# Mixture-of-experts stage: routing joined to the expert steps, first transfers reordered, output gain applied to expert rows

## What is computed

```python
x = x + g1 * mix
h = rms_norm_2(x, ffn_norm_g[layer]) * (1 + sc2) + sh2
ffn = moe(h, router_w, router_b, ex_w1[layer], ex_w3[layer], ex_w2[layer])
x = x + g2 * ffn

# in moe: 16 experts in 4 groups of 4; best group, then its best 2 experts
scores = jax.nn.sigmoid(h2 @ router_w)
...
y = (jax.nn.silu(xb @ w1[e]) * (xb @ w3[e])) @ w2[e]     # per row, 1024 -> 512 -> 1024
return y * g[:, None]                                     # gate of the row, then summed per token
```

## Time and profile before

| | us |
|---|---|
| median of three runs | 4971.45 |
| the profiled execution | 4973.66 |
| its span, first to last instruction | 4972.0 |
| routing and start of steps, layer 0 | 3304 to 3395 |
| expert steps, layer 0 | 3395 to 3887 |
| combine, layer 0 | 3887 to 3946 |
| routing and start of steps, layer 1 | 4346 to 4437 |
| expert steps, layer 1 | 4437 to 4930 |
| combine, layer 1 | 4930 to 4972 |

### The profile page before, as it was taken

How to read it: one execution, slowest core, us unless ns; L and a number is a source line. 1 busy time by engine, 2 the same in 40 slices (tenths; PEclk the granted TensorE clock), 3 DMA queues, 4 the chain that set the end, 5 groups by cost and what they waited for, 6 DMA issues and landing times. The chain is left out here.

```text
span 4972.0 us, 59425 instructions
## 1 busy us (share of the span) xinstructions
PE 4175.6 (84%) x20947; PEld 2139.8 (43%) x20947; DVE 1899.6 (38%) x2939; ACT 1138.8 (23%) x1872; POOL 261.4 (5%) x366
## 2 busy tenths in 40 slices
PE   3699699998999998999588978856999599939995
PEld 0355355555444445777444435432333244413331
DVE  1233344443312205998535837431111423321113
ACT  0122355443111112222020236210111235101111
POOL 0000000000000000111000000000000200000001
PEclk7799899999999998999799989978999799969997
DMA  6322311113355511111240130334864511266656
GB/s 254 115 67 62 69 38 38 36 36 123 120 197 207 207 57 47 53 53 52 95 155 9 55 115 26 100 141 185 327 253 167 186 29 54 98 254 241 241 228 258
DMA packets 261229, 627.23 MB, mean 126 GB/s; under 512 B 73837, under 2 KB 153789, under 8 KB 241257
## 3 DMA queue, kind: packets, MB, share of 16 engines
q1 hardware_dynamic: 222194, 508.17, 28.9%
q0 software_dynamic: 19424, 94.01, 5.1%
q10 hardware_dynamic: 19480, 23.31, 1.4%
HBM read 1298.33 MB, written 113.53 MB: 284 GB/s over the span
## 5 line engine op out<-in xcount | busy, mean ns | idle before, releaser
L3425 PE MATMUL blocks_h<-od_hT,blocks_xT 128*32 128x512 f32 x1280 | 288.3, 604 | 74.6 <-ACT blocks_xT L3368 67.5
L1645 PE MATMUL hyp_acc<-hy_hT,hyp_early_weights 128*128 128x512 f32 x768 | 335.0, 594 | 0.0
L3425 PE MATMUL blocks_h<-moe_w,blocks_xT 128*32 128x512 f32 x2560 | 295.5, 615 | 27.1 <-issue 27.1
L3446 PE MATMUL blocks_acc<-moe_w,blocks_hidT 128*32 128x512 f32 x2560 | 285.8, 598 | 10.0 <-DMA moe_w<-in_ex_w 10.0
L3425 PE MATMUL blocks_h<-moe_w1b,blocks_xT 128*32 128x512 f32 x1280 | 288.3, 604 | 0.0
L970 PE MATMUL att_scores<-att_kT,att_qT 64*128 64x512 f32 (+3 forms) x768 | 251.6, 547 | 22.2 <-DMA att_v<-scratch_V 22.2
L700 PE MATMUL lat_acc<-lat_w_in,lat_hT 128*128 128x512 f32 (+1 forms) x640 | 244.6, 538 | 2.5 <-DMA lat_w_in<-in_attn_w_in 2.5
L2209 PE MATMUL evp_acc<-ev_hT,evp_early_weights 128*128 128x512 f32 x512 | 224.6, 599 | 7.6 <-DVE evp_qkT L2350 5.6
L906 DVE TENSOR_REDUCE att_nmax<-att_scores 128x1 f32<-128x1280 f32 x128 | 190.2, 1486 | 101.9 <-PE att_scores L970 101.9
L994 PE MATMUL att_turn<-ident,att_probs 128*128 128x128 f32 x1280 | 192.1, 281 | 42.3 <-DVE att_o L936 22.5
L1645 PEld LDWEIGHTS hyp_acc<-hy_hT,hyp_early_weights 128*128 128x128 f32 x768 | 144.8, 191 | 173.7 <-issue 173.6
(11 more groups left out here) (524 smaller groups left out, 6209.4 us busy)
## 6 DMA issues: line engine op xcount, KB each, us to landing
moe_w<-in_ex_w SPq DMA_DIRECT2D x320, 2048.0 KB
od_hT<-in_ex_w SPq DMA_DIRECT2D x80, 2048.0 KB
moe_w1b<-in_ex_w SPq DMA_DIRECT2D x80, 2048.0 KB
hyp_m_weights<-in_mod_w POOLq DMA_DIRECT2D x6, 8192.0 KB, 24.2
mod_weights<-in_ada_w SPq DMA_DIRECT2D x6, 4096.0 KB, 23.3
scratch_y_rows<-blocks_y ACTq DMA_DIRECT2D x40, 512.0 KB, 8.6
hyp_early_weights<-in_hy_w_in SPq DMA_DIRECT2D x8, 2048.0 KB
scratch_parts<-hyp_uT SPq DMA_DIRECT2D x24, 512.0 KB, 3.9
```

What stands on the lines that cost most here:

```text
L1645: mm = nc.tensor.matmul(acc[:, m % 2, half * NC:(half + 1) * NC], weights[:, ws, kt, c:c + P], hT[:, kt, half * NC:(half + 1) * NC], start ...
L3425: mm = nc.tensor.matmul(out[mine, :], xT[:, kt, mine], w[l][:, kt, :], start=(kt == 0), stop=(kt == KT - 1))
L3446: mm = nc.tensor.matmul(acc[mine, c, :], hidT[:, kt, mine], w2[l][:, kt, c * NC:(c + 1) * NC], start=(kt == 0), stop=(kt == FT - 1))
```

## The change

1. `moe_route` is gone as a stage: its instructions stand at the head of `moe_blocks`' engine programs. Its tiles are carved from `xT`, `x` slot 0, `hid`, `hidT` and, as before, the last w2 lane; its PSUM from `h1`, `h3` and `hturn`.
2. DVE waits for two tables (bias, `iota`) instead of five; the constant `block_ends` and the table `steps128` are gone. The two comparisons with their sums become each three small instructions: scale and shift, then add and subtract a large constant to round.
3. SP's order: bias, `iota`, `earlier`, `token`, the three norm columns, `gain_row` (moved here from the combine stage); wait for `owned`; four lanes of w1; wait until both first row gathers have landed; four of w3; four of w2.
4. The eviction of `down` is now two DVE products with `gain_row`, one for each half, written into the `x` slot of that step; the ACT copy and the tile `y` are gone. ACT only issues the store. A row gather into a slot waits until the slot's store has landed (`y_out[s]`).
5. The combine stage has two DVE instructions for each tile, with the residual folded into the first: (y0 * gate0 + x), then (y1 * gate1 + that). The ACT product and `gain_row` are gone there. The gather for tile t+4 waits for the second instruction of tile t instead of the first of three.

```diff
@@ moe_blocks
-        y = sb("y", [P, D])
+        gain_row = sb("gain_row", [P, D])
...
+                sp.dma_start(bias, row(d["router_b_2"], P)).then_inc(first_in, 16)
+                sp.dma_start(iota, d["k_iota"]).then_inc(first_in, 16)
+                for dst, k in ((earlier, "k_earlier"), (token_no, "k_token")):
+                    sp.dma_start(dst, d[k]).then_inc(tables_in, 16)
                 for n, v in enumerate((shift, scale, norm_w)):
                     sp.dma_start(cols[:, n, :], v.rearrange("(p kt) -> p kt", kt=KT)).then_inc(cols_in, 16)
+                sp.dma_start(gain_row[:, :], row(gain, P)).then_inc(gain_in, 16)
+                sp.wait_ge(owned, signals(1))
+                each = [sp.value_load(owners[0:1, l * STEPS:l * STEPS + 1], min_val=0, max_val=EXPERTS - 1) for l in range(LANES)]
+                for m, dst in enumerate((w1, w3, w2)):
+                    if m == 1:
+                        for s in range(S):
+                            sp.wait_ge(x_in[s], 16)
+                    for l in range(LANES):
+                        load_part(sp, d, layer, dst[l], m, each[l]).then_inc(w_in[l][m], 16)
                 up_weights(1, next_experts(1))
...
                 def gather(n, s, first=False):
                     b = n * S + s
                     pool.wait_ge(token_ready, signals(b + 1))
                     if not first:
                         pool.wait_ge(turned, signals(b * 2 - 2))
+                        pool.wait_ge(y_out[s], signals(n * 16 - 16))
...
-                link(tt(more[:, :, :], wide(base[:, TT, :], MAX_PER), steps128[:, :].unsqueeze(1).to_broadcast([P, EXPERTS, MAX_PER]),
-                        ALU.is_gt))
-                link(reduce(blocks[:, :], more[:, :, :], AX.X, ALU.add))
+                link(ts(blocks[:, :], base[:, TT, :], 1.0 / MB, 0.5 - 0.5 / MB, ALU.mult, ALU.add))
+                link(ts(blocks[:, :], blocks[:, :], ROUND, None, ALU.add))
+                link(ts(blocks[:, :], blocks[:, :], ROUND, None, ALU.subtract))
...
-                link(tt(ended[:, :, :], wide(dest_f[:, :], PLACES), block_ends[:, :].unsqueeze(1).to_broadcast(by_end), ALU.is_ge))
-                link(reduce(row_block[:, :], ended[:, :, :], AX.X, ALU.add))
+                link(ts(row_block[:, :], dest_f[:, :], 1.0 / MB, 0.5 / MB - 0.5, ALU.mult, ALU.add))
+                link(ts(row_block[:, :], row_block[:, :], ROUND, None, ALU.add))
+                link(ts(row_block[:, :], row_block[:, :], ROUND, None, ALU.subtract))
...
@@ moe_blocks, result on DVE
-                    dve.wait_ge(y_out, signals(n * (16 * S) + 16 * s))
-                    nc.vector.tensor_copy(y[:, NC:], acc[:, 1, :]).then_inc(y_dve, 1)
+                    dve.wait_ge(y_out[s], signals(n * 16))
+                    for c in range(2):
+                        half = slice(c * NC, (c + 1) * NC)
+                        last = nc.vector.tensor_tensor(x[:, s, half], acc[:, c, :], gain_row[:, half], ALU.mult)
+                    last.then_inc(y_dve, 1)
@@ moe_blocks, result on ACT
-                    act.wait_ge(y_made, signals(b + 1))
-                    act.wait_ge(y_out, signals(n * (16 * S) + 16 * s))
-                    nc.scalar.activation(y[:, 0:NC], acc[:, 0, :], ACT.Copy).then_inc(y_act, 1)
-                    act.wait_ge(y_act, signals(b + 1))
                     act.wait_ge(y_dve, signals(b + 1))
-                    act.dma_start(d["y_rows"][rows_of(n, s), :], y[:, :]).then_inc(y_out, 16)
+                    act.dma_start(d["y_rows"][rows_of(n, s), :], x[:, s, :]).then_inc(y_out[s], 16)
@@ moe_combine
-                        pool.wait_ge(steps, signals(2 * (t - S) + 1))
+                        pool.wait_ge(summed, signals(t - S + 1))
...
-                    dve.wait_ge(weighted, signals(t + 1))
+                    dve.wait_ge(y_in[s], 32 * (t // S) + 32)
+                    if t >= S:
+                        dve.wait_ge(stored[s], signals(16 * (t // S)))
...
-                    link(nc.vector.scalar_tensor_tensor(out[:, s, :], y[:, s, 1, :], gate[:, 1, t:t + 1], out[:, s, :],
+                    link(nc.vector.scalar_tensor_tensor(out[:, s, :], y[:, s, 0, :], gate[:, 0, t:t + 1], x[:, t, :],
                                                         ALU.mult, ALU.add))
-                    link(nc.vector.tensor_tensor(out[:, s, :], out[:, s, :], gain_row[:, :], ALU.mult))
-                    nc.vector.tensor_tensor(out[:, s, :], out[:, s, :], x[:, t, :], ALU.add).then_inc(summed, 1)
+                    nc.vector.scalar_tensor_tensor(out[:, s, :], y[:, s, 1, :], gate[:, 1, t:t + 1], out[:, s, :],
+                                                   ALU.mult, ALU.add).then_inc(summed, 1)
```

More of the change, by code:

```diff
@@ new lines, in moe_blocks, with sequence, before, after @@
+        lanes = [slice(l * MB, (l + 1) * MB) for l in range(LANES)]
+        LAST = STEPS // S - 1
+        def sequence(eng, first, step):
+            first()
+            with eng.Fori(0, LAST) as i:
+                step(i, 1, True)
+                step(i + 1, 0, True)
+            step(LAST, 1, False)
+        def before(n, s):
+            return (n, 0) if s else (n - 1, 1)
+        def after(n, s):
+            return (n + 1, 0) if s else (n, 1)
+        assert STEPS % S == 0 and S == 2
@@ new lines, in moe_blocks @@
+        bias, iota, earlier = carve([P, EXPERTS]), carve([P, P]), carve([P, P])
+        ones, token_no = carve([P, P]), carve([P, TT])
+        scores, biased = scores_in[:, :, :].rearrange("p t (g e) -> p t g e", g=GROUPS), carve(GE)
+        hi, lo = carve([P, TT, GROUPS, 2]), carve([P, TT, GROUPS, 2])
+        top, second, low2 = (carve([P, TT, GROUPS]) for _ in range(3))
+        best, index = carve([P, TT]), carve([P, TT])
+        equal, group_hot = carve([P, TT, PER_GROUP]), carve([P, TT, GROUPS])
@@ new lines, in moe_blocks @@
+        prod, inside = carve(GE), carve([P, TT, PER_GROUP])
+        local_hot = carve([P, TT, PER_GROUP])
+        hot = [carve(GE) for _ in range(TOP)]
+        chosen = carve(GE)
+        sel, sel_sum = carve([P, TT, TOP]), carve([P, TT])
+        base = carve([P, TT + 1, EXPERTS])
+        blocks, end, start = (carve([P, EXPERTS]) for _ in range(3))
+        place = carve([P, TT, EXPERTS])
+        dest_f, row_block, lane, step_no, row_place = (carve([P, ROWS]) for _ in range(5))
+        owner, changed = carve([1, PLACES]), carve([1, PLACES])
@@ L3068, in _, with next_experts @@
             def _(sp):
[L3069 to L3073 removed]
+                def next_experts(t):
+                    at = [bass.ds(t + l * STEPS, 1) for l in range(LANES)]
+                    return [(sp.value_load(owners[0:1, a], min_val=0, max_val=EXPERTS - 1),
+                             sp.value_load(changes[0:1, a], min_val=0, max_val=1)) for a in at]
@@ new lines, in refill, with up_weights, down_weights @@
+                def refill(m, experts):
+                    for l, (one, new) in enumerate(experts):
+                        load_part(sp, d, layer, (w1, w3, w2)[m][l], m, one, new).then_inc(w_in[l][m], 16)
+                def up_weights(t, experts):
+                    for m, made in enumerate((h1_made, h3_made)):
+                        sp.wait_ge(made, signals(t))
+                        refill(m, experts)
+                def down_weights(t, experts):
+                    sp.wait_ge(y_made, signals(t))
+                    refill(2, experts)
@@ L3095, in _, with first, step @@
+                def first():
+                    gather(0, 0, True)
+                    gather(0, 1, True)
+                def step(n, s, more):
+                    if more:
+                        gather(*after(n, s))
+                sequence(pool, first, step)
             @block.vector
@@ L3306, in column @@
+                link(nc.vector.tensor_copy(tokens[:, :], table[:, :]))
                 def column(n, s):
@@ L3511, in _ @@
             def _(sp):
-                sp.dma_start(gain_row[:, :], row(gain, P)).then_inc(gain_in, 16)
                 if norm is not None:
```

271 lines of the change are left out of this document (97 added, 174 removed).

## The result

| | before | after |
|---|---|---|
| median, us | 4973.24 | 4914.97 |
| lowest to highest of four runs | 4967.36 to 4975.05 | 4910.12 to 4917.23 |
| ratio, 95% interval | | 0.9879 (0.9867 to 0.9891) |
| profiled execution, its span | 4973.66, 4972.0 | 4910.12, 4908.1 |

The kernel became 58.3 us faster, 4915 where 4917 had been forecast. The sum inside that number is another matter: the two spans differ by 63.9 us, and split at the same instructions they come out like this. The routing runs from the router's sigmoid on ACT to SP's first weight issue, the head from there to the first product with w2, the steps from that to the end of the last product with w2.

The account below looks back on a forecast made before the run. PE bounds the whole span, but each layer's start is bound by 25 MB of weights queued ahead of the norm columns. 27.7 + 15.1 - 1.2 + 7.5 + 5.3 = 54.4 us off 4971.45 gives 4917, range 4905 to 4932.

Parts of the forecast that it names:

- the large term: Start of each layer: PE's hole behind late norm columns shrinks; gains of 27.7 us in layer 0, 15.1 in layer 1.
- The signs: Expected profile: `h_gain` before transposes, layer 0's first product about 28 us after first weight issue, no `x` wait in steps.
- What bounds the kernel: PE over the span; at each layer's start, 25 MB of weights queued ahead of the norm columns, DVE idle 45.27 us.
- Routing: Before the first weight issue: 1.4 and 0.8 us saved, 0.4 lost to the larger `begin`; issue at 3326.4 instead of 3328.22.
- Head of layer 0: First product with w2 at 3402.3 instead of 3430.01, despite a hold bubble of about 5 us; gain 27.7 us.
- Head of layer 1: Step 1 waits for two changed weight parts queued behind w2; 4458.8 against 4473.89, gain 15.1 us.
- Rival (a): Layer 0's step 1: skipped w1 refills signal only in queue order, so PE starts it later; 4926 us, chance 0.20.
- Rival (b): Head: gathers get through fast and the hold costs no bubble, 4.8 us less in each layer; 4908 us, chance 0.12.
- Steps: Expert steps: longer evictions cost 1.2 us in all; the row gather's store wait stays hidden, 25.5 us against 45.3.
- Rival (d): Steps: store-to-gather chain passes 45.3 us and lengthens each step; slower than before, 5031 us at an excess of 6, chance 0.03.
- Combine: Combine stages: fewer DVE instructions a tile gain 7.5 us in layer 0 and 5.3 in layer 1.

Follow-up runs that it names:

- Columns first: Kernel before with only the three norm column transfers moved ahead of the weights; 4937.4 us, ratio 0.9925.
- columns late: Changed kernel with only the three norm column transfers put back behind the twelve weight parts; 4958.3 us, ratio 0.9963.
- the kernel with the gather in the reload: Changed kernel with each row gather held until the rows of the block before it are transposed; 4922.8 us, ratio 0.9898.
- store-late kernel: Changed kernel with ACT issuing each block's store one step later, behind the next block's rows; 4908.9 us, ratio 0.9871.

## Why the prediction was right, and where its sum was not

The prediction had the large term right and its number by luck: the forecast sum lacks the steps' gain of some 12 us, and its heads and combine stages are too large by about 9.

**The signs.** Most came. `h_gain` is ready ahead of the transposes, layer 0's first product comes 28.1 us after the first weight issue, SP's w3 issue 25.9 us after it, and PE waits for `x` only at the two heads. Ahead of w3's products PE was idle 13.2 us, not about 10.

**What bounds the kernel.** Right. Columns first gives 40.6 us of head by itself (37 us at the median), columns late takes it all back.

**Routing.** 1.8 us a layer were forecast, 1.3 and 1.1 came. The biased scores start at 3306.62, 4.95 us after the sigmoid, before 5.47 us after it: 0.5 us and not the 1.4 - 0.4 of the sum. SP's first table issue came 2.14 us after the sigmoid (3303.81), before 1.49, so the larger `begin` costs 0.65 and not 0.4, and `iota` took 2.4 us from its issue until DVE started, not 2.2.

**Head of layer 0.** The w3 issue was forecast 25.9 us after the first weight issue and came there. What was left out is the third gather: `column(1, 0)` follows the first rows, so it is issued at 3354.71, and its 0.5 MB stand amid w3. The w3 products start 50.2 us after the first weight issue, forecast 47.8, although the bubble was 3.7 us and not 5. In the kernel with the gather in the reload, where that gather is issued only at 3387.40, they start after 48.5 us, and its head has 75.9 us, the forecast number.

**Head of layer 1.** The same gather stands in the queue here too. The w1 products of step 1 started 75.9 us after the first weight issue instead of 72.7 and, from the low clock, took 9.9 us instead of 8.8 (4403.11 to the transposes at 4413.04). The mechanism was right, the term was 4.3 us too large.

**Rival (a), skipped refills in queue order.** It is false, and the changed kernel's own trace says so: PE starts step 1 of layer 0 at 3388.62, released by `xT`, while 434 GB/s of w2 are in flight. The Trainium skill (DMA: Bandwidth & Descriptors, "Why a DMA increments its semaphore by 16 and not by 1") has the issuing sequencer write at once what no DMA engine will write; this agrees: the skipped w1 refills of step 1 were issued at 3363.18, with w3 and w2 ahead of them in the queue until about 3395, and held nothing back.

**Rival (b), fast gathers.** False: 11.2 us from the first gather's issue (3338.99) to the transposes (3350.22), beside a stream of 420 GB/s, and a bubble of 3.7 us. The Trainium skill's rule of turns between the queues (same page, "Queues, rings and completion order"), read as equal shares, gave an estimate of 4.9 us for both gathers; the trace does not agree. With less beside it the gather is much faster, 4.4 us in the median of the store-late kernel.

**Steps.** This is the term that failed. The prediction asked of the new wait only whether the rows would still be in time (25.5 against 45.3 us) and answered that rightly; the wait hides, even 17 us longer. It did not ask what the moved transfer had stood beside. In the earlier trace rows PE waited 3.70 us for weights in a stage where every microsecond of the reload is on the path, and a 0.5 MB gather ran in it. That costs in two ways. The first is in every trace: w3 comes later. 0.5 MB at 387 GB/s, the rate of that reload, are 1.4 of the 2.1 us between before and after. The second is the clock behind the longer pause. The windows of the w3 products behind the pause of 3.70 us, before, and of 1.48 us, after:

```profile
3493.60:3503.20 9.60, 9.59 (x65) 2.73 (x66) 0.00 (x0) 0.00 (x0) 0.00 (x0) 0.74 0.38 159
```

```profile
3465.80:3473.00 7.20, 7.20 (x66) 2.55 (x67) 0.03 (x1) 0.00 (x0) 0.94 (x1) 1.00 0.87 329
```

The granted clock is 0.74 on average in the first and 1.00 in the second; the products take 9.5 us and 7.1. So a wait that is 2.2 us shorter made this step 4.7 us shorter (28.85 to 24.19, from one step's first product with w2 to the next's). The clock does not follow from the pause's length alone, though. In the kernel with the gather in the reload, the same products had 1.00 and took 7.1 us behind a pause of 3.39 us:

```profile
3467.20:3474.40 7.20, 7.19 (x65) 2.55 (x66) 0.00 (x0) 0.00 (x0) 0.00 (x0) 1.00 0.61 255
```

That parts the two costs. In the steps of layer 0 that reload, PE's pauses add up to 16.9 to 18.7 us in the four traces with the gather in the reload and 10.7 to 13.9 in the other ten. What these steps take beyond 22.6 us and their pauses is 8.5 to 9.0 us in three of the four, 4.8 in the fourth, the one just shown, and 5.3 to 8.3 in the ten. The clock is also most of why layer 1 scatters: pauses of 3.44, 2.46 and 1.87 us gave steps of 28.7, 25.2 and 24.6 in one trace of the changed kernel, and 3.20, 2.96 and 2.59 gave 28.4, 28.5 and 27.0 in the other; behind the 2.46 the granted clock was 1.00, behind the 2.96 it was 0.68.

**Rival (d), the row buffer as the bound.** False with a margin: see store late.

**Combine.** Layer 0: 7.5 forecast, and 7.6 came with the longer eviction (forecast 6.9 net). That POOL holds the first tiles was expected: four of DVE's tiles follow each other at 5.0 to 5.3 us, the last two at 4.45. Layer 1: 4.7 forecast net, 2.9 came. With 415 GB/s the stage is at DMA's limit throughout, and the last gathered rows set its end:

```profile
4884.00:4902.00 18.00, 0.00 (x0) 0.00 (x0) 12.08 (x10) 0.00 (x0) 6.14 (x7) 0.50 1.02 415
```

```profile
4902.44 1.28 DVE L3587 SCALAR_TENSOR_TENSOR combine_out<-moe_w,moe_gate,moe_w1b 128x1024 f32<-128x1024 f32 x1 [1.33 <-DMA moe_w<-scratch_y_rows,moe_dest]
```

The faster DVE stores tiles earlier, beside the last gathers, so the last ones land later: the crowding was forecast at 1 us. That it is about 3 is worked out from the difference; neither this nor the reason was tested alone.

**What stays open.** What decides the clock behind PE's pauses, and whether the later store gains anything. Its steps equal those of the changed kernel's fastest execution, whose other trace has 6.0 us more in layer 1; and the stretch ahead of layer 0's sigmoid, which no edit touches, took 3295.5 to 3308.8 us in the fourteen traces, more than the 6 to 9 us in question.

## What to carry to other kernels

When a change adds a wait in front of a transfer, ask two questions: does it still arrive in time, and what did it stand beside before. A transfer that nobody waits for costs its bytes to the one that somebody does wait for, and moving it by 13 us was worth 8 us at the median in the kernel before, and 12 us by the means of the traces. At a start where PE waits for a queue, order the queue by who needs what first, small operands first of all and the next step's part ahead of this step's last; a hold in that queue costs its bubble and has to protect something that the trace shows to be late.

## What the runs showed of the hardware

A conditional transfer that moves nothing signals ahead of others that stand before it in its queue: issued at 3363.18, it had let PE go at 3388.62, with w3 and w2 coming in until about 3395. The length of PE's pause did not settle the granted clock in the products behind it: it was 1.00 behind 1.48, 2.14, 2.46 and 3.39 us, but 0.80 behind 1.90, 0.78 behind 2.01, 0.68 behind 2.96 and 0.74 behind 3.70. A gather of 0.5 MB took 11.2 us beside 420 GB/s of weights and 4.4 in the median of the store-late kernel's steps, with less beside it. The root's power on POOL, one column of 128 numbers, took 0.57 us in the first two tiles, 1.62 in the next two, where DVE worked beside it on wide rows, and 0.55 in the last four; whether DVE was the cause was not tested.
